# An activation tile 64 bytes lower against its weights, and set-up matmuls in halves, in a transformer kernel on one core

## The reference

```python
D_MODEL, SEQ, D_FF = 1024, 512, 2816

def first_block(x, ...):
    for layer in range(2):
        h = rms_norm(x, norm_mix_pre[layer])
        m = mixer_block(h, ...)
        x = x + rms_norm(m, norm_mix_post[layer])
        h = rms_norm(x, norm_ffn_pre[layer])
        f = (silu(h @ w_gate) * (h @ w_up)) @ w_down
        x = x + rms_norm(f, norm_ffn_post[layer])

def second_block(x, ...):
    x = x + 0.5 * rmsnorm(swiglu(rmsnorm(x, ffn1_pre_g), ...), ffn1_post_g)
    h = rmsnorm(x, mix_pre_g)
    ... # 8 dense heads with 2 key heads, 8 heads with dilated windows
    x = x + rmsnorm(heads @ w_out, mix_post_g)
    x = x + 0.5 * rmsnorm(swiglu(rmsnorm(x, ffn2_pre_g), ...), ffn2_post_g)
```

## Time and profile before

| | us |
|---|---|
| median of 3 runs | 2650.5 (2650.3 to 2650.63) |
| the profiled execution | 2650.62 |
| its span, first to last instruction | 2648.8 |
| PE busy | 2633.4 (99% of the span) |
| PE weight loads busy | 2369.2 |
| DVE busy | 1914.5 (72%) |
| ACT busy | 1332.4 (50%) |

### The profile page before, as it was taken

One profiled execution on the slowest core, in us unless ns is written; L12 is line 12 of the kernel. 1 busy time (PEld: TensorE's weight loads), 2 busy tenths in 40 slices (PEclk: granted clock), 3 DMA queues, 4 the chain that ended last, 5 costly groups with the idle time before them and its releaser, 6 DMA issues.

```text
span 2648.8 us, 42168 instructions
## 1 busy us (share of the span) xinstructions
PE 2633.4 (99%) x17164; PEld 2369.2 (89%) x17164; DVE 1914.5 (72%) x2711; ACT 1332.4 (50%) x2008; POOL 57.0 (2%) x59
## 2 busy tenths in 40 slices
PE   9999999999999999999999999999999999999998
PEld 7888999899988888899989998999988877899987
DVE  6956877688854785687678893588854798688843
ACT  5345644455642534654465562455633467455631
POOL 0020000000000003000000000000000000000000
PEclk9999999999999999999999999999999999999999
DMA  4242332333333324233333333233333430233332
GB/s 152 80 117 75 119 104 80 120 117 103 101 110 90 112 80 129 63 120 105 116 99 112 104 94 110 76 120 108 98 104 93 122 103 2 72 120 112 96 107 77
DMA packets 77216, 266.23 MB, mean 101 GB/s; under 512 B 9600, under 2 KB 12032, under 8 KB 76128
## 3 DMA queue, kind: packets, MB, share of 16 engines
q1 hardware_dynamic: 71136, 254.87, 31.4%
q10 hardware_dynamic: 5888, 8.68, 1.3%
HBM read 251.71 MB, written 4.19 MB: 97 GB/s over the span
## 4 chain that ended last, share of the span: by engine, by line
PE 97%; DVE 1%; ACT 1%; issue 0%; DMA 0%; ACTq 0%; SPq 0%; DVEq 0%; POOL 0%; POOLq 0%
PE bank L515 30%; PE bank L517 29%; PE bank L516 29%; PE bank L2061 1%; PE bank L2039 1%; PE bank L1773 1%; PE bank L2025 1%; PE bank L1789 1%; DVE w_lo L701 0%; PE bank L1829 0%; PE bank L1807 0%; ACT w_hi L697 0%; PE bank L582 0%; PE bank L590 0%; DVE x L867 0%
## 5 line engine op out<-in xcount | busy, mean ns | idle before, releaser
L515 PE MATMUL bank<-u_hi,w_hi 128*128 128x256 f32 (+1 forms) x2352 | 759.2, 323 | 1.7 <-DVE w_lo L701 1.1
L517 PE MATMUL bank<-u_hi,w_lo 128*128 128x256 f32 (+1 forms) x2352 | 749.3, 319 | 0.0
L516 PE MATMUL bank<-u_lo,w_hi 128*128 128x256 f32 (+1 forms) x2352 | 748.4, 318 | 0.0
L701 DVE TENSOR_TENSOR w_lo<-raw,w_hi 128x1024 fp32r<-128x1024 f32 x250 | 310.8, 1247 | 330.8 <-ACT w_hi L697 330.4
L515 PEld LDWEIGHTS bank<-u_hi,w_hi 128*128 128x128 f32 x2352 | 446.9, 190 | 38.3 <-issue 4.1
L516 PEld LDWEIGHTS bank<-u_lo,w_hi 128*128 128x128 f32 x2352 | 446.9, 190 | 32.4 <-issue 2.4
L517 PEld LDWEIGHTS bank<-u_hi,w_lo 128*128 128x128 f32 x2352 | 446.9, 190 | 31.3
L697 ACT ACTIVATE w_hi<-raw 128x1024 fp32r<-128x1024 f32 x250 | 263.3, 1055 | 335.0 <-PE bank L517 248.4
L515 PE MATMUL bank<-cm,w_hi 128*128 128x256 f32 x1152 | 319.5, 277 | 0.0
L516 PE MATMUL bank<-cm,w_hi 128*128 128x256 f32 x1152 | 319.0, 277 | 0.0
L517 PE MATMUL bank<-cm,w_lo 128*128 128x256 f32 x1152 | 318.6, 277 | 0.0
(11 more groups left out here) (358 smaller groups left out, 4374.7 us busy)
## 6 DMA issues: line engine op xcount, KB each, us to landing
raw<-in_weights SPq DMA_DIRECT2D x314, 512.0 KB, 3.6
rx<-in_weights SPq DMA_DIRECT2D x72, 512.0 KB, 3.5
xr<-in_weights SPq DMA_DIRECT2D x48, 512.0 KB, 3.5
raw<-in_weights SPq DMA_DIRECT2D x32, 384.0 KB, 3.1
rot_s<-rot_in ACTq DMA_DIRECT2D x32, 128.0 KB, 2.3
q_s<-q_in ACTq DMA_DIRECT2D x52, 64.0 KB, 3.3
x<-in_x SPq DMA_DIRECT2D x4, 512.0 KB, 7.0
ret_mask<-in_ret_mask SPq DMA_DIRECT2D x2, 1024.0 KB, 6.3
```

Source lines behind the costliest of these rows:

```text
L515: nc.tensor.matmul(out, st_hi, mv_hi, start=first, stop=False, skip_group_check=onto)
L516: nc.tensor.matmul(out, st_hi, mv_lo, start=False, stop=False, skip_group_check=onto)
L517: return nc.tensor.matmul(out, st_lo, mv_hi, start=False, stop=last, skip_group_check=onto)
L701: nc.vector.tensor_tensor(w_lo[:, bl.slot(p), :], raw[:, bl.raw(p), :], w_hi[:, bl.slot(p), :].bitcast(F32), ALU.subtract).then_inc(lo_spl ...
```

## The change

- A third pair of names for the same space: `uf_hi` and `uf_lo` lie where `u_hi` and `u_lo` were. Everything behind them (`u_hi`, `u_lo`, `raw`, the weights, all tiles further on) moves up by 64 bytes. So the offset of `uf` from the weights is 192 modulo 256, and that of `u`, `cm`, `gm`, `hid` is as it was.
- The four feed-forward stages and the heads of the attention stage use `uf`; the mixers and the attention's own products keep `u`. The output of a feed-forward stage is gathered in the pair that the next stage reads.
- The two set-up matmuls of 512 columns become eight of 256 (two banks, two halves, twice), with `uf_hi` both moving and stationary.

```diff
+        ahead_at = top[0]
+        top[0] += LINE - MOVING_AT
         u_hi_at = top[0]
         u_hi = place("u_hi", [P, KD, T], F32R)
         u_lo = place("u_lo", [P, KD, T], F32R)
+        uf_hi = place("uf_hi", [P, KD, T], F32R, ahead_at)
+        uf_lo = place("uf_lo", [P, KD, T], F32R, ahead_at + 4 * KD * T)
...
-        ffn_out = place("ffn_out", [P, KD, T], F32, u_hi_at)
+        out_to_mix = place("out_to_mix", [P, KD, T], F32, u_hi_at)
+        out_to_ffn = place("out_to_ffn", [P, KD, T], F32, ahead_at)
...
+        def u_of(s):
+
+            return (uf_hi, uf_lo) if s in FFN_STAGES else (u_hi, u_lo)
...
-            for b in (OUT_B, OUT_C):
-                nc.tensor.matmul(ps[FIRST_BANK + b][:, :], u_hi[:, 0, 0:P], u_hi[:, 0, :], start=True, stop=True)
+            for again in range(SET_TWICE):
+                for b in (OUT_B, OUT_C):
+                    for cols in (LEFT, RIGHT):
+                        nc.tensor.matmul(ps[FIRST_BANK + b][:, cols], uf_hi[:, 0, 0:P], uf_hi[:, 0, cols], start=again == 0 and cols == LEFT,
+                                         stop=True, skip_group_check=True)
...
-            pe_block(pe, bl, 3, ou, 3, u_hi, u_lo, each_k=sums_k)
+            pe_block(pe, bl, 3, ou, 3, uf_hi, uf_lo, each_k=sums_k)
             for i in range(N_UP, N_LEAD):
-                pe_block(pe, bl, i, ou, i, u_hi, u_lo)
+                pe_block(pe, bl, i, ou, i, uf_hi, uf_lo)
...
+            ffn_out = out_to_ffn if s + 1 in FFN_STAGES else out_to_mix
```

More of the change, by code:

```diff
@@ L47 @@
 HALF = P // 2
+FFN_STAGES = (1, 3, 4, 6)
+SET_TWICE = 2
 LINE = 256
@@ L605, in pe_first @@
             beside = s in FIRST_NO
+            in_hi, in_lo = u_of(s)
             if s in (1, 3):
@@ L620, in add @@
                     w = slice(k * P, (k + 1) * P)
-                    mm = three(to[:, cols], w_hi[:, b, w], w_lo[:, b, w], u_hi[:, k, cols], u_lo[:, k, cols],
+                    mm = three(to[:, cols], w_hi[:, b, w], w_lo[:, b, w], in_hi[:, k, cols], in_lo[:, k, cols],
                                k == K_ORDER[0], k == K_ORDER[-1])
@@ L710, in act_pre @@
                 act.wait_ge(x_ready.sem, x_ready.upto(s, hf * KD + i + 1))
-                nc.scalar.activation(u_hi[:, k, cols], x[:, k, cols], ACT.Copy, scale=gains[:, k:k + 1]).then_inc(u_hi_ev.sem, 1)
+                nc.scalar.activation(u_of(s)[0][:, k, cols], x[:, k, cols], ACT.Copy, scale=gains[:, k:k + 1]).then_inc(u_hi_ev.sem, 1)
                 if hf == 1:
@@ L797, in dve_low @@
             cols, k = token_half(hf), K_ORDER[i]
+            to_hi, to_lo = u_of(s)
             dve.wait_ge(u_hi_ev.sem, u_hi_ev.upto(s, hf * KD + i + 1))
-            nc.vector.scalar_tensor_tensor(u_lo[:, k, cols], x[:, k, cols], gains[:, k:k + 1],
-                                           u_hi[:, k, cols].bitcast(F32), ALU.mult, ALU.subtract).then_inc(u_lo_ev.sem, 1)
+            nc.vector.scalar_tensor_tensor(to_lo[:, k, cols], x[:, k, cols], gains[:, k:k + 1],
+                                           to_hi[:, k, cols].bitcast(F32), ALU.mult, ALU.subtract).then_inc(u_lo_ev.sem, 1)
         def dve_first(dve, gains, k):
@@ L936, in st_moving @@
             if i == 0:
-                return u_hi[:, k, LEFT], u_lo[:, k, LEFT]
+                return uf_hi[:, k, LEFT], uf_lo[:, k, LEFT]
             if i == 3:
-                return u_hi[:, KH + k, LEFT], u_lo[:, KH + k, LEFT]
+                return uf_hi[:, KH + k, LEFT], uf_lo[:, KH + k, LEFT]
             if i == 5:
-                return u_hi[:, KH + k, RIGHT], u_lo[:, KH + k, RIGHT]
+                return uf_hi[:, KH + k, RIGHT], uf_lo[:, KH + k, RIGHT]
             c = {1: N1, 2: MINUS_Z, 4: T3, 6: T4}[i]
@@ L2080, in _ @@
             for i in range(KD - 2):
-                pe_block(pe, bl, N_QKV + i, ou, E_SCORE + 64 + i, u_hi, u_lo, each_k=heads_k if i == 0 else None)
-            pe_project_end(pe, bl, N_QKV + KD - 2, ou, E_SCORE + 64 + KD - 2, u_hi, u_lo, "post3", 5)
+                pe_block(pe, bl, N_QKV + i, ou, E_SCORE + 64 + i, uf_hi, uf_lo, each_k=heads_k if i == 0 else None)
+            pe_project_end(pe, bl, N_QKV + KD - 2, ou, E_SCORE + 64 + KD - 2, uf_hi, uf_lo, "post3", 5)
             bl, ou = bl.on(N_QKV + KD), ou.on(E_SCORE + 64 + KD)
@@ L2483, in _ @@
                     act.wait_ge(use.filled, use.n + 1)
-                    nc.scalar.activation(u_hi[:, g, :], use.mem[:, :], ACT.Copy).then_inc(hd_hi.sem, 1)
+                    nc.scalar.activation(uf_hi[:, g, :], use.mem[:, :], ACT.Copy).then_inc(hd_hi.sem, 1)
             for m in range(KD - 2):
@@ L3086, in head_low @@
                 dve.wait_ge(hd_hi.sem, hd_hi.upto(0, g + 1))
-                nc.vector.tensor_tensor(u_lo[:, g, :], use.mem[:, :], u_hi[:, g, :].bitcast(F32), ALU.subtract).then_inc(use.drained, 1)
+                nc.vector.tensor_tensor(uf_lo[:, g, :], use.mem[:, :], uf_hi[:, g, :].bitcast(F32), ALU.subtract).then_inc(use.drained, 1)
             for p in range(-2, 33):
```

## The result

| | before | changed |
|---|---|---|
| median, us | 2650.3 (2650.04 to 2650.63, 5 runs) | 2664.61 (2664.29 to 2665.08, 5 runs) |
| ratio | | 1.0054 (1.0043 to 1.0065) |
| span of the profiled execution, us | 2648.8 | 2662.4 |

The change makes the kernel 14.3 us slower, where 16.7 us less was forecast. In the changed kernel lines 526 to 528 are `three`, 975 is the set-up, 593 the sums of block 3, 709 `w_hi`, 713 `w_lo`, 826 `acc`, 1362 `hid_lo`.

A forecast was written before the change was run, and what follows sets the result against it. PE's distance between matmul starts was taken as the bound. Four feed-forward stages at 3.7 + 0.7 − 0.5 = 3.9 us (15.4 together) and 1.3 in the projection make 16.7 off 2650.62: 2633.9, range 2631 to 2644.

The forecast's parts named there:

- rival A: Strassen part: `uf` stages entered slow stay at 117.8 ns; all four 2661, one 2640; chance 0.08 (one or two), 0.07 (three or four).
- The pitch of `uf` at 256 columns, 171.3 us: Set-up to down projection: 1512 matmuls at 113.3 ns take 171.3 us in place of 175.7, a gain of 4.4.
- What is kept, 0.66 waited again at k = 2: First down block: PE waits 0.66 us again for DVE's `hid_lo`, so 3.7 us of the gain is kept.
- `pe_first`, 0: Its 144 matmuls before the sums gain nothing, since PE waits there for DVE's `acc`; bounds 0 and 0.9 us a stage.
- 512 columns, 220 ns: Blocks 3 to 7 behind the sums: 102 matmuls at 220 ns in place of 226.7, 0.7 us gained a stage.
- Set-up, 0.5: Ahead of the Strassen part: eight matmuls of 256 columns for two of 512 cost 0.5 us more a stage.
- The projection, −1.3: Attention's projection up to its sums: 144 matmuls of 512 and 57 of 256 columns gain 1.3 us.
- The rest, 0: Other tiles keep their offset, and 64 bytes in absolute place change nothing; bounds ± 1 us.
- D: All tiles: absolute address counts, so `cm` and `gm` lose while `hid`, `mg` and mixer's `u` win; about 2636, chance 0.03.
- B: Strassen products: the offset does nothing for `u`, only the longer set-up stays; 2652.6, chance 0.10.
- C: Blocks ahead of set-up and projection: the offset helps 256 columns but not 512; 2637.6, chance 0.10.

The follow-up runs named there:

- e9: PE alone, no transformer: six set-ups, each behind 512-column matmuls at offset 192 entered six ways; the 256-column matmuls after them took 113.3 or 117.8 ns.
- e5: The changed kernel with six matmuls at offset 0 against the weights in place of its set-up; 2639.5 us, ratio 0.9958.
- e7: The changed kernel, set-up kept, with blocks 3 to 7 computed by halves of 256 columns; 2664.35 us.
- e4: The changed kernel with 24 matmuls at offset 0 against the weights in place of its set-up; 2647.95 us.
- e10: The changed kernel with three matmuls at offset 0 against the weights in place of its set-up; ten executions from 2637.01 to 2656.41 us.
- e1: PE alone, no transformer: streams of matmuls at offsets 0 to 224 from the weights; at 192, 113.3 ns for 256 columns and 233.3 for 512.
- e3: The kernel before with only the eight new set-up matmuls, on `u`; 2652.32 us, 2.0 more than before.
- e2: The changed kernel with the two old set-up matmuls of 512 columns, on `uf`; ten executions in steps from 2638.5 to 2662.87 us.
- e6: The changed kernel with its set-up once, four matmuls in place of eight; ten executions in steps from 2638.05 to 2656.55 us.
- e8: The changed kernel with blocks 3 to 7 and the attention's projection by halves, and six matmuls at offset 0 for a set-up; 2638.39 us.
- e11: The changed kernel with blocks 3 to 7 and projection by halves, three matmuls at offset 0 behind the sums and three for set-up; 2636.3 to 2643.95 us.
- e12: The changed kernel with blocks 3 to 7 and projection by halves, three matmuls at offset 0 behind the sums, six for set-up; 2638.69 us, ratio 0.9954.

## Why the prediction was wrong, step by step

The step that failed is in rival A. The prediction had found both pitches of offset 192, said that nothing would put a slow stage back, and priced that; then it set the case aside, because "eight matmuls at offset 0 ahead of it are what the kernel before has in each `u` product", and gave three or four slow stages 0.07. It took `uf` on itself as the same thing as `u` against the weights. It isn't. Eight on itself left 117.8 from every pattern (six entries in e9, four stages of the changed kernel); six against the weights left 113.3 from every pattern (six entries, four stages of e5). The two differ in number as well as in kind, and eight against the weights were not run. But in e7 the eight on itself ran at a steady 120 ns up to the last, as the 24 against the weights did in e4 from the tenth on, and what followed took 117.8 in all four stages of the one and 113.3 in all four of the other. That speaks for the kind. The pitches inside the set-up would not have told: 124, 118, 116, 119, 119, 121, 116 ns in the changed kernel, 112, 118, 118, 117, 120, 120 for the six behind P in e9 and 116, 118, 120, 120, 117, 118 behind R. The rule that offset 0 puts the pitch back, read from products of 24 matmuls of 256 columns, held for those and for six of them; it does not hold for three (e9, e10), nor for 24 of 512 columns (e1), and the set-up was not an instance of it. What the row of the one slow `gm` product gave was a state that depends on what came before, and a forecast resting on such a state needs a row of the very entry that it will have. There was none, so 0.07 was too sure.

Point by point:

1. *The pitch of `uf` at 256 columns, 171.3 us.* Right as what offset 192 can give: 171.38 in e5. In the change it was 178.08, the figure of rival A (178.1).
2. *What is kept, 0.66 waited again at k = 2.* Right: the load is 0.67 late in e5, of which the matmuls lose 0.57, and from the first `hid` matmul to the next stage's sums 144.31 us where 143.73 stood before. In the change there is no such wait, because PE is late.
3. *`pe_first`, 0.* Right in the main: the load is 0.12 us behind `acc`, and PE waits up to 0.71 us there. But "PE already waits there for DVE" misread the row: the matmul itself was not late in the kernel before, and so the place could give back a part. From the sums of the mixer ahead, stages 1 and 3 reach theirs 0.2 and 0.4 us earlier in the changed kernel.
4. *512 columns, 220 ns.* Wrong in sign. The step is "offset 0 costs the same overhead at both lengths, and so the part that goes should be the same". Offset 0 is the best for 512 columns (e1), 192 costs 233.3, outside the bounds of 220 and 226.7. So +0.67 a stage in place of −0.7, 5.5 us for the four.
5. *Set-up, 0.5.* Right: e3 gave 2.0 for four.
6. *The projection, −1.3.* Wrong by the same step: 144 matmuls of 512 columns at 233.3 lose 1.0, the 57 of 256 that run at 113.4 give 0.4 back, and from the sums of this stage to those of the next it came out 0.1 longer (the waits behind take up some): 1.4 off.
7. *The rest, 0.* Right. `hid` and the mixers keep their pitch, which also rules out D.

With points 4 and 6 at their measured size the forecast is 2633.9 + 5.5 + 1.4 = 2640.8 for eight matmuls that reset; for six, four times 0.24 less, 2639.8. e5 measured 2639.5. Rival A's 2661 becomes 2664.6 with point 4 mended (it had counted −0.24 a stage where +0.67 came, four times 0.9 more). The change measured 2664.6; that it is the same to 0.1 is in part luck, since A's −0.5 for the projection, where +0.1 came, would add 0.6, and the mixer stages ahead were 0.6 shorter.

B is ruled out by e1 and e5; C had the gain at 256 columns right and the price at 512 as a bound that was passed.

**What stays open.** What draws the pattern at the entry of a stage: five kernels with the same instructions up to there had three patterns. The traces narrow it to the sums of block 3. In all 24 stages of the six kernels that differ in the set-up alone (the changed one, e2, e4, e5, e6, e10), the last pitches ahead of the sums are 236 and 231 in the same order, within 1 ns; behind the sums, where PE waited between 0.01 and 0.74 us, any of the three patterns follows. Which wait leads to which was not tried. If Q is what makes e2 and e10 slow, its share was 25 of 40 stages in the one and 9 of 40 in the other, which no run explains. Nor does a run show what inside the chip the offset and the patterns are.

## What to carry to other kernels

Where PE is the bound, measure the distance of starts for each pair of moving and stationary tile and for each number of columns: an offset that gains 6.7 ns at 256 columns can lose 6.6 at 512, so give it only to the tiles whose matmuls gain. A pitch that is lower in some rows can be one of two states; before a change takes away the matmuls that put it back, find which entries lead to which, in a stream of PE alone, and keep a reset that works from all of them (here six matmuls of 256 columns at offset 0 with `w_hi` and `w_lo` stationary, 0.7 us). A kernel whose executions fall on evenly spaced times may be drawing such a state. The step divided by the number of matmuls in a stage says how much pitch to look for: here 6.15 us by 1512 is 4.1 ns, and the pitches differ by 4.4.

## What the hardware showed that was not expected

- The pitch of float32 matmuls depends on the offset between moving and stationary tile modulo 256 bytes, and the order of the offsets is another one for 256 columns (113.3 at 192, 120.0 at 0) than for 512 (226.7 at 0, 233.3 at 192, up to 234.2 at 160). It is the offset between the two and not the address: in the changed kernel `hid` and the weights both lie 64 bytes higher, and `hid` keeps its 226.7 at 512 columns.
- Offset 192 has at least two steady states at 256 columns (113.3 and 117.8, held for 1512 matmuls) and three patterns at 512 (233, 233, 234; 231 and 236 in either order), all at the same granted clock.
- Matmuls that come between carry the state on by rules of their own: two, four and eight matmuls of a tile on itself each map the three patterns in another way.
- The Trainium skill, page "PSUM — Partial Sum Buffer", section "The four PSUM rules", has it that two accumulation groups open at once in the same bank can't both carry the first-matmul flag, since the second clears what the first has set. The halves of e7 and e8 both carry it, and by that rule the left half is overwritten where it should be added to; e11 and e12 carry it on the left half alone. No row of a trace shows the flag.
